# Three products of high and low parts as two matmuls: the down projections and the up projections of two SwiGLU stages

## The chip, the cores and the metric

The kernel runs on one core of a Trainium2 chip. The metric is the device time of one execution in microseconds (us), lower is better. The time before is the median of three runs, 1114.51 us (1113.62 to 1114.54).

## The reference, cut to what matters

One sequence of 256 tokens with 1024 features passes through three layers. Each ends in a feed-forward stage of width 2816 (22 blocks of 128):

```python
def conv_ffn(h, w_up, conv_w, conv_b, w_down):      # first layer: stage "1"
    a = causal_dwconv(h @ w_up, conv_w, conv_b)
    gate, val = jnp.split(a, 2, axis=-1)
    return (jax.nn.silu(gate) * val) @ w_down
def swiglu(h, w_gu, w_down):                        # second and third layer: stages "a" and "b"
    gate, up = jnp.split(h @ w_gu, 2, axis=-1)
    return (jax.nn.silu(gate) * up) @ w_down
```

All is float32. Ahead of the second layer's feed-forward stage stands its mixer, `x + concat([grouped, mem_out]) @ w_out`; its output product is called "outa" here.

## The kernel before, in words

Everything is kept feature-major: an array is [128 partitions, chunk of 128 features, 256 tokens]. Weights stream from HBM through four slots of a ring (`ring`, 1 MB each) on SyncE's queue (SP). The order of all work is one list of steps made by `order()` and walked by every engine: ("g", stage, i) is one group of a projection, 256 outputs wide, which fills one PSUM bank of 512 float32 columns (two halves of 128 outputs x 256 tokens); ("sq", ...), ("ns", ...) and ("nm", ...) are the squares, the sums over features and the reciprocal root of a norm.

**The split products.** For most projections a float32 product is made of three matmuls in the type float32r. A weight W is split into W_hi (ScalarE copies it with rounding, `high`, L1444) and W_lo = W - W_hi (VectorE, `low`, L1865), in halves of 1024 columns; two buffers of each (`w_hi`, `w_lo`) alternate. The activations have `xh`, `xl` in the same way. `three` (L938) then issues for each chunk k of 128 input features W_hi x_hi, W_hi x_lo and W_lo x_hi, each a matmul of 256 columns with a weight load of its own, all accumulated in the same 256 columns of PSUM. Call the three of one k a triple. ScalarE may overwrite buffer q%2 with weights q+2 only when the group that used q has ended (`grouped`), and TensorE starts group q+2 when VectorE has made its low part (`lo_ready`).

**The up products (`ffn`).** 22 groups in each stage: per group two halves (gate, value) of 8 triples. A group uses one of the four banks `banks[g % RING]`. VectorE then multiplies the bank by the norm's reciprocal root (L2257, 128x512, into `acc`), makes the next low weights, and in stages "a" and "b" waits for ScalarE's silu of the gate half (L1748), multiplies gate and value (L2280), rounds the product to `hid_hi` (L2283) and subtracts for `hid_lo` (L2285). In stage "1" GpSimd does these last three and VectorE does a convolution. The other four banks (S0, S1, T, O) serve scores, transposes, attention outputs and norm sums, and are idle in the feed-forward stages but for the norm's sums.

**The down products** (stage[:4] == "down"): 8 groups in each of the three stages, each of 22 triples in two halves of the weights (11 chunks, 128x1408), in 256 columns of a bank; VectorE adds the bank to x (L2060).

**outa** has four groups. They are not split: `feature_major` (L986) runs plain float32 matmuls on `mixa` and the ring's slot; each leaves two records of 256 columns in the trace. Group 0 is begun early.

**Norm sums.** VectorE adds the squares of four pairs of chunks to `total` (L2107, 128x512), folds the two halves of `total` together (L2111, 128x256), and TensorE multiplies by ones once (L1213).

Of the kernel before, what the change touches and what calls it, by code (L numbers as in the profile page):

```python
# [30 lines left out]
P = 128  # L31
# [214 lines left out]

BRANCHES = ("fox", "mla")
# [9 lines left out]
def order():  # L257
# [37 lines left out]
    st += [("row", "fox", 0), ("row", "fox", 1), ("g", "memkv", 1), ("keep",), ("nm", "m5"), ("sq", "m6")]  # L295
# [31 lines left out]
    def first_layer(heads):  # L327


        n = len(heads)  # L330
        out = [("G", *heads[0])]
        made, conv = [], []
        for t in range(n + 2):
            ssd = t < n and heads[t][0] == "ssd"
            ends = [heads[h] for h in (t - 2, t - 1) if h in range(n) and heads[h][1] % 2 and
                    (heads[h][0] == "ssd") == (h == t - 1)]
            out += starts(heads, t) + ([("B", *heads[t])] if ssd else [])
            out += [("sh", *g) for g in made[-1:]] + [("tn", *g) for g in conv]
            out += [("D", *h) for h in ends]
            out += [("C", *heads[t - 1])] if 1 <= t <= n else []  # L340
            out += [("B", *heads[t])] if t < n and not ssd else []
            out += [("sl", *g) for g in made[-1:]]
            out += [("P", *heads[t])] if t < n and not ssd else []
            out += [("fn", *g) for g in conv]
            out += [("L", *h) for h in ends if h[0] in BRANCHES]
            out += [("ev", *g) for g in made]
            out += [("G", *heads[t + 1])] if t + 1 < n else []
            conv = [g for g in made if g[0] == "xbc"]
            made = [g for g in dense[t] if len(g) == 2 and g[0] in TICKED]
            for g in dense[t]:  # L350
                if g[0] not in TICKED:
                    out.append(g)
                elif len(g) == 3:
                    out.append(("half", *g[:2]))
                else:
                    out.append(("g", *g))
                    if g != made[-1]:
                        out += [("sh", *g), ("sl", *g)]
            out += [("row", "ssd" if t else "fox", h) for h in rows_at.get(t, ())]
            out += {0: [("nm", "m6"), ("sq", "m7")], 1: [("nm", "m7")]}.get(t, [])  # L360
            for i, at in enumerate((26, 28, 30, 33)):
                if t == at:
                    out += [("hi", "ssm", i), ("sq", "ssm", i)] + ([("ns", "ssm", i)] if i < 3 else [])
        return out
# [8 lines left out]
    pool = [[("g", "pool", 1)], [("g", "pool", 0), ("pl", 0), ("g", "memkv", 2)], [("g", "wg", 2)], [("g", "wg", 1)],  # L373
            [("g", "wg", 0), ("early",)], [("g", "memkv", 3)]]
# [35 lines left out]
def number(steps):  # L410
# [4 lines left out]
    def one(stage, i):  # L415
        nonlocal g, l
        group[stage, i] = g
        key = load_key(stage, i)
        keys = [(stage, 2 * i), key] if stage[:4] == "down" else [key]
        for key in keys:  # L420
            if key not in load:
                load[key] = l
                l += 1
                if stage in SPLIT or stage[:2] == "up" or stage[:4] == "down":
                    split[key] = len(split)
            last[key] = g
        g += 1
# [96 lines left out]
def build(nc, cst_at, par_at, x_in, mem_in, pos_in, cst_in, cst2_in, par_in, w, out):  # L524
    with ExitStack() as ctx:
# [13 lines left out]
        xh = sb("xh", [P, KC, S], F32R)  # L539
        xl = sb("xl", [P, KC, S], F32R)  # L540
# [76 lines left out]
        hid_hi = zb("hid_hi", [P, NFF, S], F32R)  # L617
        hid_lo = zb("hid_lo", [P, NFF, S], F32R)
# [19 lines left out]
        zb("hole5", [P, (2 * NFF - 14) * S - 6 * 16])  # L638
# [54 lines left out]
        tapped = sem("tapped")  # L693
        stored = sem("stored")
# [103 lines left out]
        def halves_of(wide):  # L798
            return (0, wide // 2), (wide // 2, wide)

# [96 lines left out]
        def _(pe):  # L897
# [30 lines left out]
            def three(out, w_of, x_of, ks, wait=None, stationary=True, whole=True, start=True, **kw):  # L928


                for k in ks:
                    if wait is not None:
                        pe.wait_ge(*wait(k))
                    for a, b in ((0, 0), (0, 1), (1, 0)):
                        lhs, rhs = w_of(a, k), x_of(b, k)
                        if not stationary:
                            lhs, rhs = rhs, lhs
                        last = mm(out, lhs, rhs, start=(start and k == 0 and (a, b) == (0, 0)), **kw,  # L938
                                  stop=(whole and k == ks[-1] and (a, b) == (1, 0)))
                return last  # L940
# [103 lines left out]
            def group(stage, i, half=None):  # L1044
# [36 lines left out]
                elif stage[:4] == "down":  # L1081
                    base = FFN_BASE[stage[4]]
                    hidden = lambda k: (up_hid, base + k + 1)
                    for half in range(2):
                        parts = split_parts((stage, 2 * i + half))
                        last = three(banks[g % RING][:, 0:S],
                                     lambda a, k: parts[a][:, (k % HALF) * P:(k % HALF + 1) * P],
                                     lambda a, k: (hid_hi, hid_lo)[a][:, k, :],
                                     range(half * HALF, (half + 1) * HALF),
                                     hidden if i == 0 else None, whole=half == 1)  # L1090
# [52 lines left out]
                elif stage == "outa":  # L1143
# [4 lines left out]
                    else:  # L1148
                        last = feature_major(stage, i, W, KC, 256, two, lambda k: mixa[:, k, :])
# [18 lines left out]
            def ffn(name):  # L1168
                g0, q0 = GROUP["up" + name, 0], SPLITS["up" + name, 0]

                def up(u, it):
# [3 lines left out]
                    W = w_hi[:, q % 2, :], w_lo[:, q % 2, :]  # L1175
                    w_of = lambda m, a, k: W[a][:, k * 256 + m * P:k * 256 + (m + 1) * P]
# [8 lines left out]
                    last.then_inc(grouped, 1)  # L1185

# [8 lines left out]
            def total_sums(s):  # L1195
# [16 lines left out]
                pe.wait_ge(folded, n["totals"])  # L1212
# [206 lines left out]
        def _(act):  # L1419
# [296 lines left out]
            def ffn(name):  # L1716
                conv = name == "1"
                g0, n0, q0 = GROUP["up" + name, 0], LOAD["up" + name, 0], SPLITS["up" + name, 0]

                def up(j, u, it):  # L1720
# [13 lines left out]

                    parts()
                    act.wait_ge(free, it + (g // RING + 1))
# [34 lines left out]
            for s in STEPS:  # L1771
# [4 lines left out]
                elif s[0] == "tn":  # L1776
                    xbc_tanh(s[2])
                elif s[0] == "rest":
# [61 lines left out]
        def _(dve):  # L1840
# [127 lines left out]
            def group(stage, i):  # L1968
# [127 lines left out]
            def add_squares(name, i):  # L2096
# [12 lines left out]
                if i == 3:  # L2109
# [128 lines left out]
            def ffn(name):  # L2238
# [4 lines left out]
                def up(j, u, it):  # L2243
# [13 lines left out]
                    V.tensor_tensor(y.rearrange("p (a t) -> p a t", a=2), bank[:, :].rearrange("p (a t) -> p a t", a=2),  # L2257
                                    factor(S), ALU.mult).then_inc(free, 1)
# [28 lines left out]
                with dve.Fori(0, NFF // RING) as it:  # L2287
# [11 lines left out]
            for s in STEPS:  # L2299
# [4 lines left out]
                elif s[0] == "fn":  # L2304
                    xbc_finish(s[2])
                elif s[0] == "rest":
# [70 lines left out]
        def _(pool):  # L2377
# [25 lines left out]
            def up(j, u, it):  # L2403
# [4 lines left out]
                pool.wait_ge(up_silu, it * RING + (u + 1))  # L2408
                Q.tensor_tensor(h, sg[:, r, 0:S], acc[:, r, S:2 * S], ALU.mult).then_inc(hid_t, 1)  # L2409
                pool.wait_ge(hid_t, it * RING + (u + 1))  # L2410
                Q.tensor_copy(hi, h).then_inc(hid_high, 1)
                pool.wait_ge(hid_high, it * RING + (u + 1))
                Q.tensor_tensor(lo, h, hi, ALU.subtract).then_inc(up_hid, 1)

            for s in STEPS:
                if s[0] == "G":
                    decays(s)
                elif s == ("ffn", "1"):
                    with pool.Fori(0, NFF // RING) as it:
                        for u in range(RING):  # L2420
                            up(it * RING + u, u, it)
# [31 lines left out]
```

## Time and profile before

| what | value |
|---|---|
| median of three runs | 1114.51 us |
| the profiled execution's own time | 1113.32 us |
| its span, first to last instruction | 1111.5 us |
| TensorE busy | 1088.2 us (98%) |
| VectorE busy | 767.8 us (69%) |
| ScalarE busy | 599.5 us (54%) |
| GpSimd busy | 97.5 us (9%) |
| mean load of the DMA engines over the span | 172 GB/s |
| granted TensorE clock, mean | 0.997 |

Busy times are unions of spans in which an engine had an instruction under way. A matmul's own duration contains its fill and drain and overlaps its neighbours', so what one matmul costs is the distance from its start to the start of the next (its pitch), not the mean duration in a group's row. The chain is the work that ended last, followed back from the end of the program.

### The profile page before, as it was taken

To read this page: it belongs to the slowest core of one execution; us is meant where nothing else is said; L and a number is where in the kernel's file an instruction comes from. 1 tells how busy PE (TensorE), PEld (TensorE's weight loads), DVE (VectorE), ACT (ScalarE), POOL (GpSimd) and SP (SyncE) were. 2 spreads that over 40 slices of the span, in tenths; PEclk is the share of its full clock that TensorE was granted. 3 is DMA by queue.
4 is the path that set the end of the run, shared out by engine and by line. 5 is a ranking of instruction groups with operands and counts; after the bars stand their busy time and mean duration, and the time that the engine had idled before them with its cause. 6 is when DMAs were issued, how large, how long until landed. Compare 5 with 4: busy or idle time off the path is not lost.

```text
span 1111.5 us, 21454 instructions
## 1 busy us (share of the span) xinstructions
PE 1088.2 (98%) x8622; PEld 1039.4 (94%) x8622; DVE 767.8 (69%) x1213; ACT 599.5 (54%) x948; POOL 97.5 (9%) x112
## 2 busy tenths in 40 slices
PE   8999999999999999999999999999999999999997
PEld 8987899999999999999978999999999779999997
DVE  6855898678877999955744677756656446777643
ACT  6675667556646556544423444436657644444353
POOL 0000211055200433200000000000000000000000
PEclk9999999999999999999999999999999999999999
DMA  9445443556545556456524655445643136554451
GB/s 343 151 166 202 155 157 105 177 181 217 169 173 175 178 186 232 148 179 219 176 76 154 243 182 186 162 156 188 227 171 115 39 114 228 190 189 165 157 185 62
DMA packets 33905, 191.07 MB, mean 172 GB/s; under 512 B 3917, under 2 KB 7269, under 8 KB 16677
## 3 DMA queue, kind: packets, MB, share of 16 engines
q1 hardware_dynamic: 33252, 188.95, 48.7%
q10 hardware_dynamic: 576, 1.05, 0.3%
q8 instruction: 55, 0.90, 0.3%
q14 instruction: 22, 0.17, 0.0%
HBM read 187.86 MB, written 2.12 MB: 171 GB/s over the span
## 4 chain that ended last, share of the span: by engine, by line
PE 87%; DVE 7%; ACT 4%; issue 1%; DMA 1%; SPq 0%; DVEq 0%; ACTq 0%
PE bank L938 73%; PE bank L986 5%; DVE w_lo L1865 2%; PE bank L995 1%; PE O L1340 1%; ACT w_hi L1444 1%; PE S L1226 1%; PE bank L1020 1%; PE T L1313 1%; PE bank L1030 1%; ACT pr L1683 1%; DVE padu L1950 1%; DMA x<-x_in 1%; PE O L1345 0%; PE S L1248 0%
## 5 line engine op out<-in xcount | busy, mean ns | idle before, releaser
L1444 ACT ACTIVATE w_hi<-ring 128x1024 fp32r<-128x1024 f32 (+2 forms) x348 | 316.6, 957 | 329.7 <-PE bank L938 329.7
L938 PE MATMUL bank<-xh,w_hi 128*128 128x256 f32 x1600 | 452.9, 283 | 2.4 <-DVE w_lo L1865 1.6
L1865 DVE TENSOR_TENSOR w_lo<-ring,w_hi 128x1024 fp32r<-128x1024 f32 (+2 forms) x348 | 372.9, 1113 | 117.3 <-ACT w_hi L1444 116.4
L938 PE MATMUL bank<-xl,w_hi 128*128 128x256 f32 x1600 | 447.3, 280 | 0.0
L938 PE MATMUL bank<-xh,w_lo 128*128 128x256 f32 x1600 | 445.7, 279 | 0.0
L938 PEld LDWEIGHTS bank<-xh,w_hi 128*128 128x128 f32 x1600 | 300.6, 188 | 6.0 <-issue 4.2
L938 PEld LDWEIGHTS bank<-xl,w_hi 128*128 128x128 f32 x1600 | 300.9, 188 | 0.2
L938 PEld LDWEIGHTS bank<-xh,w_lo 128*128 128x128 f32 x1600 | 300.7, 188 | 0.0
L938 PE MATMUL bank<-hid_hi,w_hi 128*128 128x256 f32 x528 | 148.2, 281 | 0.5 <-DVE w_lo L1865 0.5
L938 PE MATMUL bank<-hid_lo,w_hi 128*128 128x256 f32 x528 | 148.1, 280 | 0.0
L938 PE MATMUL bank<-hid_hi,w_lo 128*128 128x256 f32 x528 | 148.1, 280 | 0.0
L938 PEld LDWEIGHTS bank<-hid_hi,w_hi 128*128 128x128 f32 x528 | 99.5, 188 | 0.7 <-issue 0.7
L938 PEld LDWEIGHTS bank<-hid_hi,w_lo 128*128 128x128 f32 x528 | 99.5, 188 | 0.0
L938 PEld LDWEIGHTS bank<-hid_lo,w_hi 128*128 128x128 f32 x528 | 99.5, 188 | 0.0
L2257 DVE TENSOR_TENSOR acc<-bank,rstd 128x512 f32<-128x512 f32 x44 | 30.4, 692 | 42.4 <-PE bank L938 35.4
L2267 DVE SCALAR_TENSOR_TENSOR acc<-pr,par,acc 128x255 f32<-128x255 f32 (+1 forms) x88 | 56.5, 681 | 3.0 <-DVE acc L2267 0.2
L1565 ACT ACTIVATE xh<-x,cst,par 128x256 fp32r<-128x256 f32 x40 | 21.8, 592 | 38.2 <-DVE x L2063 32.7
L2086 DVE SCALAR_TENSOR_TENSOR xl<-x,par,xh 128x256 fp32r<-128x256 f32 x40 | 17.6, 481 | 18.8 <-ACT xh L1565 18.8
L2409 POOL TENSOR_TENSOR sg<-sg,acc 128x256 f32<-128x256 f32 x20 | 17.1, 853 | 135.9 <-ACT sg L1753 135.9
L2063 DVE SCALAR_TENSOR_TENSOR x<-bank,x 128x512 f32<-128x512 f32 x12 | 8.3, 688 | 28.0 <-PE bank L1030 14.2
L2400 POOL TENSOR_SCALAR G<-mqk,sums 128x256 f32<-128x256 f32 x12 | 18.1, 1512 | 85.8 <-ACT pr L1660 49.2
L1742 ACT ACTIVATE acc<-pr,par 128x256 f32<-128x256 f32 x44 | 23.8, 588 | 0.0
(327 smaller groups left out, 1561.3 us busy)
## 6 DMA issues: line engine op xcount, KB each, us to landing
ring<-w_up SPq DMA_DIRECT2D x22, 1024.0 KB, 4.9
ring<-w_upa SPq DMA_DIRECT2D x22, 1024.0 KB, 4.8
ring<-w_upb SPq DMA_DIRECT2D x22, 1024.0 KB, 4.8
ring<-w_gate SPq DMA_DIRECT2D x12, 1024.0 KB, 4.9
ring<-w_down SPq DMA_DIRECT2D x16, 704.0 KB, 4.0
ring<-w_downa SPq DMA_DIRECT2D x16, 704.0 KB, 4.0
ring<-w_downb SPq DMA_DIRECT2D x16, 704.0 KB, 4.0
ring<-w_xbc SPq DMA_DIRECT2D x6, 1024.0 KB, 4.9
```

The source lines that it names most:

```text
L938: last = mm(out, lhs, rhs, start=(start and k == 0 and (a, b) == (0, 0)), **kw, stop=(whole and k == ks[-1] and (a, b) == (1, 0)))
L986: last = mm(b[p0:p0 + width, m * S:m * S + S], W[0:kp, k * wide + c0:k * wide + c0 + width], src(k), start=(k == 0), stop=(k == kc - 1))
L995: last = mm(b[:, tt * wide:(tt + 1) * wide], src(k)[:, tt * P:(tt + 1) * P], W[:, k * wide:(k + 1) * wide], start=(k == 0), stop=(k == kc ...
L1444: A(w_hi[:, q % 2, a:e], raw[:, a:e], ACT.Copy).then_inc(hi_ready, 1)
L1565: last = A(hi[:, c, :], src[:, c, :], ACT.Identity, bias=C("zero"), scale=Pm(gain, c))
L1742: last = A(acc[:, r, m * S:(m + 1) * S], pr[:, r, m * S:(m + 1) * S], ACT.Identity, bias=par[:, bass.ds(j * 8 + o + 3, 1)], scale=par[:, b ...
L1865: last = V.tensor_tensor(w_lo[:, q % 2, a:e], raw[:, a:e], w_hi[:, q % 2, a:e], ALU.subtract)
L2086: last = stt(lo[:, c, :], norm_io(name)[0][:, c, :], Pm(gain, c), hi[:, c, :], ALU.mult, ALU.subtract)
L2257: V.tensor_tensor(y.rearrange("p (a t) -> p a t", a=2), bank[:, :].rearrange("p (a t) -> p a t", a=2), factor(S), ALU.mult).then_inc(free, 1)
L2267: ins = stt(part, y[:, m * S:(m + 1) * S - late], par[:, bass.ds(j * 8 + o, 1)], part, ALU.mult, ALU.add)
L2400: Q.tensor_scalar(g[:, 0:S], R, c0, 0.0, ALU.add, ALU.min)
L2409: Q.tensor_tensor(h, sg[:, r, 0:S], acc[:, r, S:2 * S], ALU.mult).then_inc(hid_t, 1)
```

## The change

1. `two_wide` is new. For each k it issues one matmul W_hi [x_hi | x_lo] of 512 columns into a whole bank (x_hi's product in columns 0 to 255, x_lo's in 256 to 511), and one W_lo x_hi of 256 columns, accumulated on columns 0 to 255. The two halves of the bank are added behind it. `xh`, `xl` and `hid_hi`, `hid_lo` become halves of one array each. The down products of all stages and the up products of stages "a" and "b" use it.
2. An up group of stages "a" and "b" now needs two banks, one for each half: `banks[g % RING]` and `second_bank(u)` = (T, O, S0, S1)[u]. ScalarE copies columns 256 to 511 of both to `pr` (two copies, ahead of its next high weights), VectorE adds columns 0 to 255 of both to `pr` (two adds into `acc`) and then multiplies by the norm's factor. `down` gets a second add into x.
3. outa's groups 1 to 3 become split products with `three`; `mixa` gets `mixa_h` and `mixa_l` (new steps "mh": a copy on ScalarE, a subtraction on VectorE), and the three weights are split as others are.
4. The fold of `total` is left out for the norms ssm, ffn1 and mixb: TensorE sums two products instead of one. The squares and sums of norms m5, m6, m7 move ahead of a group of weights each.

```diff
+THREE = [("outa", i) for i in range(1, 4)]
+FOLDED = ("x1", "mem", "mixa", "ffna", "ffnb")
@@ order
-    st += [("row", "fox", 0), ("row", "fox", 1), ("g", "memkv", 1), ("keep",), ("nm", "m5"), ("sq", "m6")]
+    st += [("nm", "m5"), ("sq", "m6"), ("row", "fox", 0), ("row", "fox", 1), ("g", "memkv", 1), ("keep",)]
...
+            out += {0: [("nm", "m6"), ("sq", "m7")], 1: [("nm", "m7")]}.get(t, [])
             conv = [g for g in made if g[0] == "xbc"]
             made = [g for g in dense[t] if len(g) == 2 and g[0] in TICKED]
...
-            out += {0: [("nm", "m6"), ("sq", "m7")], 1: [("nm", "m7")]}.get(t, [])
...
-    pool = [[("g", "pool", 1)], [("g", "pool", 0), ("pl", 0), ("g", "memkv", 2)], [("g", "wg", 2)], [("g", "wg", 1)],
-            [("g", "wg", 0), ("early",)], [("g", "memkv", 3)]]
+    pool = [[("g", "pool", 1)], [("g", "pool", 0), ("pl", 0), ("g", "memkv", 2)], [("g", "wg", 2)], [("g", "wg", 1), ("mh", 2)],
+            [("g", "wg", 0), ("early",), ("mh", 1)], [("mh", 0), ("g", "memkv", 3), ("mh", 3)]]
@@ tensor
+            def two_wide(bank, w_of, x2_of, ks, wait=None, whole=True):
+                main, both = bank[:, 0:S], bank[:, :].rearrange("p (b t) -> p b t", b=2)
+                for k in ks:
+                    if wait is not None:
+                        pe.wait_ge(*wait(k))
+                    mm(both, w_of(0, k), x2_of(k), start=k == 0, stop=False, skip_group_check=True)
+                    last = mm(main, w_of(1, k), x2_of(k)[:, 0, :], start=False, stop=whole and k == ks[-1],
+                              skip_group_check=True)
+                return last
@@ down
-                        last = three(banks[g % RING][:, 0:S],
...
+                        last = two_wide(banks[g % RING],
+                                        lambda a, k: parts[a][:, (k % HALF) * P:(k % HALF + 1) * P],
+                                        lambda k: hid[:, :, k, :], range(half * HALF, (half + 1) * HALF),
+                                        hidden if i == 0 else None, whole=half == 1)
@@ outa
-                        last = feature_major(stage, i, W, KC, 256, two, lambda k: mixa[:, k, :])
+                        pe.wait_ge(mixa_lo, 4)
+                        last = feature3(stage, i, 256, two3, None, (mixa_h, mixa_l))
@@ norm sums
-                pe.wait_ge(folded, n["totals"])
+                if name not in FOLDED:
+                    pe.wait_ge(sq_added, 3 * n["totals"])
+                    product(sums_bank(name)[:, 0:S], [(C("ones"), total[:, c * S:(c + 1) * S]) for c in range(2)])\
+                        .then_inc(s_done, 1)
+                    return
@@ scalar, up
+                    if not conv:
+                        act.wait_ge(grouped, it * RING + (g + 1))
+                        for m, b in enumerate((bank, second_bank(u))):
+                            last = A(pr[:, r, m * S:(m + 1) * S], b[:, S:2 * S], ACT.Copy)
+                        last.then_inc(rest_copied, 1)
                     parts()
...
+                        act.wait_ge(scaled, it * RING + (base - NFF + u + 1))
@@ vector, down
-                    V.tensor_tensor(x[:, i, :], x[:, i, :], b[:, 0:S], ALU.add).then_inc(free, 1)
+                    own(V.tensor_tensor(x[:, i, :], x[:, i, :], b[:, 0:S], ALU.add))
+                    V.tensor_tensor(x[:, i, :], x[:, i, :], b[:, S:2 * S], ALU.add).then_inc(free, 1)
@@ vector, up of stages a and b
+                        dve.wait_ge(rest_copied, it * RING + (base - NFF + u + 1))
+                        if not (isinstance(j, int) and j < 2):
+                            dve.wait_ge(hid_t, it * RING + (base + u - 1))
+                        for m, b in enumerate((bank, second_bank(u))):
+                            last = V.tensor_tensor(y[:, m * S:(m + 1) * S], b[:, 0:S], pr[:, r, m * S:(m + 1) * S], ALU.add)
+                        last.then_inc(free, 1)
+                        dve.wait_ge(free, it + (g // RING + 1))
+                        y2 = y.rearrange("p (a t) -> p a t", a=2)
+                        V.tensor_tensor(y2, y2, factor(S), ALU.mult).then_inc(scaled, 1)
                     parts()
```

## Rows read from the trace of the kernel before

**Rows 1.** The page: busy time by engine; the chain that ended last, by line

```profile
PE 1088.2 (98%) x8622; PEld 1039.4 (94%) x8622; DVE 767.8 (69%) x1213; ACT 599.5 (54%) x948; POOL 97.5 (9%) x112
PE bank L938 73%; PE bank L986 5%; DVE w_lo L1865 2%; PE bank L995 1%; PE O L1340 1%; ACT w_hi L1444 1%; PE S L1226 1%; PE bank L1020 1%; PE T L1313 1%; PE bank L1030 1%; ACT pr L1683 1%; DVE padu L1950 1%; DMA x<-x_in 1%; PE O L1345 0%; PE S L1248 0%
```

**Rows 2.** Chain in order of time: start us, length us, what, instructions

```profile
47.38 0.86 PE S L1226 x2
...
588.96 20.72 PE bank L986 x96
...
615.72 181.39 PE bank L938 x1536
```

**Rows 3.** Timeline, stage a's up: start us, duration us, engine, instruction

```profile
639.93 0.28 PE L938 MATMUL bank<-xh,w_hi 128*128 128x256 f32 x1
639.94 0.19 PEld L938 LDWEIGHTS bank<-xl,w_hi 128*128 128x128 f32 x1
640.05 0.28 PE L938 MATMUL bank<-xl,w_hi 128*128 128x256 f32 x1
```

**Rows 4.** Timeline of weight loads around float32 matmuls of 128 columns (L1305, L1306)

```profile
822.54 0.41 PEld L1305 LDWEIGHTS S<-pr,cst 128*128 128x128 f32 x2
822.87 0.30 PEld L1306 LDWEIGHTS S<-pr,cst 128*128 128x128 f32 x2
823.09 0.19 PEld L938 LDWEIGHTS bank<-xh,w_hi 128*128 128x128 f32 x1
823.20 0.19 PEld L938 LDWEIGHTS bank<-xl,w_hi 128*128 128x128 f32 x1
```

**Rows 5.** Timeline, VectorE in stage a's up, one whole group and the next's start

```profile
649.67 0.69 DVE L2257 TENSOR_TENSOR acc<-bank,rstd 128x512 f32<-128x512 f32 x1 [0.86 <-PE bank L938]
650.77 2.36 DVE L1865 TENSOR_TENSOR w_lo<-ring,w_hi 128x1024 fp32r<-128x1024 f32 x2 [0.40 <-ACT w_hi L1444]
653.05 0.42 DVE L2280 TENSOR_TENSOR sg<-sg,acc 128x256 f32<-128x256 f32 x1
653.62 0.29 DVE L2283 CAST hid_hi<-sg 128x256 f32 x1 [0.16 <-DVE sg L2280]
654.04 0.42 DVE L2285 TENSOR_TENSOR hid_lo<-sg,hid_hi 128x256 f32 x1
655.33 0.69 DVE L2257 TENSOR_TENSOR acc<-bank,rstd 128x512 f32<-128x512 f32 x1 [0.86 <-PE bank L938]
```

**Rows 6.** Timeline, VectorE at the start of the stage, without waits between

```profile
617.05 0.69 DVE L2257 TENSOR_TENSOR acc<-bank,rstd 128x512 f32<-128x512 f32 x1 [3.53 <-ACT rstd L1636]
...
621.57 0.42 DVE L2285 TENSOR_TENSOR hid_lo<-sg,hid_hi 128x256 f32 x1
621.91 0.68 DVE L2257 TENSOR_TENSOR acc<-bank,rstd 128x512 f32<-128x512 f32 x1
622.56 2.36 DVE L1865 TENSOR_TENSOR w_lo<-ring,w_hi 128x1024 fp32r<-128x1024 f32 x2
```

**Rows 7.** Timeline, ScalarE in the same group as rows 5, and at the stage's start

```profile
618.75 1.28 ACT L1748 ACT_TABLE_LOAD   x1
...
649.67 2.01 ACT L1444 ACTIVATE w_hi<-ring 128x1024 fp32r<-128x1024 f32 x2 [3.25 <-PE bank L938]
651.59 0.49 ACT L1748 ACTIVATE sg<-acc,cst 128x256 f32<-128x256 f32 x1
```

**Rows 8.** By line, ns min/median/max: the down add; ScalarE's copy of 256 PSUM columns

```profile
L2060 DVE TENSOR_TENSOR x<-x,bank x24: 410/414/422, 477.8 to 1103.2; 128x256 f32<-128x256 f32 x24
...
L1714 ACT ACTIVATE mixa<-O x2: 384/384/384, 567.9 to 578.5; 128x256 f32<-128x256 f32 x2
```

**Rows 9.** Timeline and chain: m5's sums, the next scores; the fold of ffn1's sum

```profile
107.06 1.02 PE L1226 MATMUL S<-sqr,cst 96*128 96x512 f32 x2
108.91 0.49 PE L1287 MATMUL S<-fqk 64*128 64x128 f32 x4 [0.82 <-issue]
...
345.72 0.43 DVE lnv L2111
```

More of the change, by code:

```diff
@@ L423, in one @@
                 l += 1
-                if stage in SPLIT or stage[:2] == "up" or stage[:4] == "down":
+                if stage in SPLIT or key in THREE or stage[:2] == "up" or stage[:4] == "down":
                     split[key] = len(split)
@@ L1185, in up, with wide_up @@
                     last.then_inc(grouped, 1)
+                def wide_up(u, it, g, w_of):
+                    begin = isinstance(it, int) and it == 0
+                    after_t, after_s = (T_USE["rt",], S_USE["nm", "mixb"]) if name == "a" else \
+                        (len(T_USE), S_USE["nm", "last"])
+                    if begin and u == 0:
+                        pe.wait_ge(t_free, after_t)
+                    if begin and u == 1:
+                        pe.wait_ge(headed, O_USE["mema" if name == "a" else "memb", 1] + 1)
+                    if begin and u >= 2:
+                        pe.wait_ge(s_free[u - 2], (after_s - u + 3) // 2)
+                    both = banks[g % RING], second_bank(u)
+                    step = 2 if begin and u == 0 else KC
+                    for k0 in range(0, KC, step):
+                        for m in range(2):
+                            last = two_wide(both[m], lambda a, k: w_of(m, a, k), lambda k: xhl[:, :, k, :],
+                                            range(k0, k0 + step), after("ffn" + name) if step == 2 and m == 0 else None,
+                                            whole=k0 + step == KC)
+                    last.then_inc(grouped, 1)
+                    if step == 2:
+                        total_sums(("ns", "ffn" + name, 3))
                 for u in range(RING):
@@ L1777, in _ @@
                     xbc_tanh(s[2])
+                elif s[0] == "mh":
+                    if s[1] == 3:
+                        act.wait_ge(headed, O_USE["mema", 1] + 1)
+                    else:
+                        g = GROUP["wg", s[1]]
+                        act.wait_ge(evacuated[g % RING], g // RING + 1)
+                    A(flat(mixa_h[:, 2 * s[1]:2 * s[1] + 2, :]), flat(mixa[:, 2 * s[1]:2 * s[1] + 2, :]), ACT.Copy)\
+                        .then_inc(mixa_hi, 1)
                 elif s[0] == "rest":
@@ L2285, in hidden @@
                     V.tensor_tensor(lo, h, hi, ALU.subtract).then_inc(up_hid, 1)
-                with dve.Fori(0, NFF // RING) as it:
+                if not conv:
+                    for j in range(RING):
+                        up(j, j, 0)
+                with dve.Fori(0 if conv else 1, NFF // RING) as it:
                     for u in range(RING):
@@ L2305, in _ @@
                     xbc_finish(s[2])
+                elif s[0] == "mh":
+                    n["mixa"] += 1
+                    dve.wait_ge(mixa_hi, n["mixa"])
+                    V.tensor_tensor(pair(mixa_l, s[1]), pair(mixa, s[1]), pair(mixa_h, s[1]), ALU.subtract)\
+                        .then_inc(mixa_lo, 1)
                 elif s[0] == "rest":
```

51 lines of the change are left out of this document (33 added, 18 removed).

## The prediction

> **What bounds the kernel now.** I read the busy times and the chain first: TensorE is busy for 98% of the span, and 73% of the chain is the one line that issues the split products [rows 1]. Nothing but TensorE time, or a new wait of TensorE, can move the end much. Then I asked what one matmul costs. The chain in order of time has a piece of 181.39 us with 1536 matmuls of 256 columns, stage a's up and down products without a break [rows 2]: 181.39/1536 = 118.1 ns each, 354.3 ns for a triple and 48 x 118.1 = 5.66 us for an up group, the 5.66 us between VectorE's groups [rows 5].
>
> 256 columns at 2.4 GHz are 106.7 ns, so 11.4 ns of each 118.1 are something else, and the case turns on what. The timeline shows that a weight load starts when the matmul before it starts (639.94 beside 639.93), and the next matmul 0.12 us later [rows 3]: as if the load, not the columns, set the pitch. Two more rows bear on it. outa's float32 matmuls leave two records each, 20.72/96 = 215.8 ns a record, 213.3 of them columns, so where the load has time to hide only 2.5 ns are lost [rows 2]. The same holds for 512 columns: 0.86/2 = 430 ns against 426.7 [rows 2]. And loads under float32 records of 106.7 ns follow each other every (823.20 - 822.87)/3 = 110 ns [rows 4]. I read: pitch = the larger of columns + 2.5 ns and one load, 110 to 118 ns, and the load is 118 beside a float32r stream.
>
> **The pair.** Per k the change streams the same 768 columns with two loads for three. By that reading the 512-column matmul takes the 215.8 ns of a record with 213.3 ns of columns (its successor's load is hidden), and the 256-column one, over which the next load must run, 118.1. Pair 333.9 ns, saved 354.3 - 333.9 = 20.4 ns. There are 22 x 8 x 3 = 528 triples in the down products and 22 x 2 x 8 x 2 = 704 in the two up stages. Down: 10.8 us. Up: 14.4 us if TensorE stays the bound there; its group becomes 16 x 333.9 = 5.34 us. Bounds per k: nothing saved (everything grows with columns) and 28.5 ns (215.8 + 110).
>
> **VectorE in the up stages.** It now has 0.86 + 0.40 us idle in 5.66 [rows 5]. Its slot of new work, from starts without waits between: last subtraction to the next instruction 0.34, rounded to 0.40 for three waits computed there [rows 6]; two adds of 256 columns, which last as long as the down add, 0.41 [rows 8], at pitch 0.34 and then, since the multiplication waits for the second, 0.57 as between L2280 and L2283 [rows 5]; the multiplication of 512 columns 0.65 [rows 6]; both low parts 2.28 (653.05 - 650.77), then 0.57 and 0.42 for the hidden block [rows 5]. Sum 0.40 + 0.34 + 0.57 + 0.65 + 2.28 + 0.57 + 0.42 = 5.23 us, against 5.34 of TensorE. It fits with 0.1 us to spare. The wait for ScalarE's copies (two of 0.38 [rows 8], so 0.8 us after a group's end) costs nothing while VectorE is still in the group before at that moment: 0.8 + 5.23 = 6.03 ends 0.69 into the next, which it may start at 0.8. Low weights are ready 0.8 + 0.34 + 0.57 + 0.65 + 2.28 = 4.6 us after the group two before them ended, TensorE wants them at 5.34. The cover is thin; at a loop's end VectorE has more bookkeeping, and I take 0.7 us off for groups in which it is late. ScalarE has 2.01 + 0.49 of 5.66 [rows 7], plus 0.8: no bound. The second banks are idle in these stages: nothing.
>
> **Starts of the two up stages.** Low weights for group 2 were ready at 617.05 + 0.77 + 2.28 = 620.1 [rows 6] and TensorE's group 1 ended at 615.72 + 5.66 = 621.4 [rows 2]. New: copies 0.8, adds 0.9, so about 621.8, and group 1 ends at 621.1. The silu's table load of 1.28 us [rows 7] keeps VectorE's backlog. In stage a the weights of group 1 can be split only after outa's last group, because outa's groups now hold both buffers: ready some 6.3 us after its end, against a first group of 5.34 and the sums. I take 1.3 us lost for both stages; bounds 0 and 3.
>
> **outa.** 48 matmuls of 431.7 ns [rows 2] become 48 triples of 354.3: 3.7 us saved. Copies and subtractions for `mixa`, and the splits of three weights (2.01 us on ScalarE, 2.28 on VectorE each), lie beside the second layer's memory-value product (memkv 3) and outa 0, ten us in which both engines are nearly idle; the last pair waits for the attention's output and is done some 2 us after that product ends, 1.5 us before group 1. Nothing, and if that cover went, 1 us.
>
> **Small parts.** After m5's sums (107.06 + 0.86) TensorE stands until 108.91, 1.0 us [rows 9]; moved ahead of a group, the wait is hidden. m6 and m7 may give as much each, or move their wait elsewhere: I take 1.5 for the three, bounds -1 and 3. The fold that ffn1 loses (0.43 [rows 9]) stands before low weights for which TensorE waits: 0.4. In the other two norms the second product of 0.43 fills TensorE's idle time: nothing. The second down add (0.41 and a wait) shows only at the program's end, partly under TensorE's first sums: 0.3 lost; in the 23 others it lies under a group of 7.8 us.
>
> **Sum.** 10.8 + 14.4 - 0.7 - 1.3 + 3.7 + 1.5 + 0.4 - 0.3 = 28.5 us. The profiled execution took 1113.3 us (span 1111.5), 1.2 below the median; the same 28.5 off the median gives **1086.0 us**. About 0.2% (2.2 us) can be told from no change.
>
> **Rivals.**
> A, a fixed 11.4 ns for every float32r matmul whatever its length: the pair is 320 + 22.8 = 342.8, saved 11.4 x 1232 = 14.0; with the rest (3.7 + 1.9 - 0.3) and 1.0 for starts, 18.3: 1096.2. For it: no float32r matmul in the trace has another length. Against it: the float32 records lose only 2.5. Chance 0.15.
> B, the extra grows with columns but for 2.5 ns: a float32r stream reads slower than 2.4 GHz. The pair is 351.8, saved 2.5 x 1232 = 3.1; in all 7.9: 1106.6. Against it only that loads and starts go in step [rows 3]. Chance 0.08. The Trainium skill, page "TensorE: Matmul & The Clock Gate", section "Back-to-back issue gap", speaks for so small a gain: it puts a warm matmul at columns/2.4 ns + 2.5 with nothing for the load, so two instead of three save 2.5 ns. Its 109.2 ns for 256 columns disagree with the 118.1 measured here.
> C, VectorE becomes the bound of the up stages: four more waits at some 0.1 us each that don't hide would make its slot 5.65, and the up products gain nothing: 10.8 + 3.7 + 1.6 - 2.0 = 14.1: 1100.4. For it: 0.1 us to spare. Chance 0.15.
> D, slower: VectorE waits in every group for ScalarE's copies and does all its work behind them, slot 0.8 + 5.23 + 0.1 = 6.1 us; 44 x (6.1 - 5.66) = 19.4 lost against 14.1 gained elsewhere: 1119.8. It decides from a slot of 5.66 + 14.1/44 = 5.98. Against it: TensorE's next group runs while VectorE works, so the copies are made in VectorE's shadow. Chance 0.05.
>
> **The numbers.** Forecast 0.54, A 0.15, B 0.08, C 0.15, D 0.05, and 0.03 for less still than all bounds. Low end: pair of 326, down 528 x 28.5 = 15.0, up held by VectorE at 5.25, 44 x 0.41 - 2 = 16.0, and 5.3 for the rest: 36.3, so 1078. High end: C and A inside, B and D left out: 1103. Faster 0.91, same 0.03, slower 0.06.
>
> **What would show it.** In the profile after: a 512-column float32r matmul and the start after it 0.216 us apart, the next pair's start 0.118 later; 342.8 in sum would be A, 352 B. Up groups 5.34 us apart on TensorE without waits for w_lo; C shows as such waits and VectorE over 98% busy at a longer period; D as VectorE waiting for ScalarE's `pr` in each group. Down groups of 22 x 0.334 = 7.35 us instead of 7.79. outa's three groups 17.0 us instead of 20.7. The prediction is wrong if the pair doesn't cost 334, or VectorE's slot exceeds 5.34.

## The result and the profile after

The changed kernel takes 1108.26 us (median of five runs, 1107.72 to 1108.64) against 1114.54 us for the kernel before (five runs on the same chip, 1113.62 to 1115.53): ratio 0.9942, 95% interval 0.993 to 0.9955, 6.3 us less. The forecast was 1086.0 in 1078 to 1103. The direction is right, the size is not: 6.3 us came for 28.5.

The page of the changed kernel, the lines that answer to [rows 1], and three of its groups of instructions (count | busy us, mean ns | idle before, what ended it):

```profile
PE 1080.5 (98%) x7444; PEld 980.5 (89%) x7444; DVE 815.1 (74%) x1332; ACT 632.8 (57%) x1046; POOL 98.7 (9%) x112
...
L960 PE MATMUL bank<-hid,w_hi 128*128 128x512 f32 x528 | 184.9, 394 | 3.3 <-DVE w_lo L1938 2.9
L961 PE MATMUL bank<-hid,w_lo 128*128 128x256 f32 x528 | 147.8, 280 | 0.0
...
L2339 DVE TENSOR_TENSOR acc<-bank,pr 128x256 f32<-128x256 f32 x44 | 18.7, 425 | 26.8 <-ACT pr L1793 26.8
```

TensorE is still busy 98% of the span. 1178 matmul records fewer stand in it (8622 to 7444: the third matmuls of 1232 triples, while outa's exchange adds 48 and the norms' second products 6), and the span is 5.6 us shorter (1105.9 against 1111.5). So 1178 fewer matmuls brought little, and the first question is what the new pair costs. The timeline of stage a's up answers to [rows 3]:

```profile
640.14 0.39 PE L960 MATMUL bank<-xhl,w_hi 128*128 128x512 f32 x1
640.14 0.19 PEld L961 LDWEIGHTS bank<-xhl,w_lo 128*128 128x128 f32 x1
640.37 0.28 PE L961 MATMUL bank<-xhl,w_lo 128*128 128x256 f32 x1
640.37 0.19 PEld L960 LDWEIGHTS bank<-xhl,w_hi 128*128 128x128 f32 x1
640.49 0.39 PE L960 MATMUL bank<-xhl,w_hi 128*128 128x512 f32 x1
```

The wide matmul starts at 640.14, the narrow one at 640.37, the next wide one at 640.49. By the medians over the stage that is 228 and 118 ns (229 to 230 and 117 in the down stages), and from pair to pair 346.7 ns on average in all five stages. The narrow one is as forecast. The wide one is 12 to 14 ns dearer than the 215.8 forecast, though the load under it (0.19 us, begun with it) ended before it did. The triples of the same stages took 353.3 ns in stage a's up, 350.0 in stage b's, and 356.0, 356.0 and 352.0 in the down products of stages 1, a and b. So the pair saves 6.7 and 3.3 ns in up and 9.3, 9.3 and 5.3 in down, not 20.4.

The timeline of VectorE in the same stage, the answer to [rows 5]:

```profile
639.74 0.42 DVE L2339 TENSOR_TENSOR acc<-bank,pr 128x256 f32<-128x256 f32 x1 [0.45 <-ACT pr L1793]
640.08 0.41 DVE L2339 TENSOR_TENSOR acc<-O,pr 128x256 f32<-128x256 f32 x1
640.52 0.69 DVE L2343 TENSOR_TENSOR acc<-acc,rstd 128x512 f32<-128x512 f32 x1
641.13 2.35 DVE L1938 TENSOR_TENSOR w_lo<-ring,w_hi 128x1024 fp32r<-128x1024 f32 x2
643.41 0.42 DVE L2365 TENSOR_TENSOR sg<-sg,acc 128x256 f32<-128x256 f32 x1
643.97 0.29 DVE L2368 CAST hid<-sg 128x256 f32 x1
644.40 0.43 DVE L2370 TENSOR_TENSOR hid<-sg,hid 128x256 f32 x1
645.19 0.42 DVE L2339 TENSOR_TENSOR acc<-bank,pr 128x256 f32<-128x256 f32 x1 [0.37 <-ACT pr L1793]
```

From 639.74 to 645.19 less 0.37 of idle time is a slot of 5.08 us; the groups come every 5.55 us. VectorE waits 0.4 us in each of these two groups. TensorE waits for low weights only at stage a's second group (below), nowhere further inside these stages.

The second finding is in the down stages, where TensorE waited only at the start before. The timeline of TensorE in the changed kernel's stage 1 down, where a first half of weights ends:

```profile
503.12 0.39 PE L960 MATMUL bank<-hid,w_hi 128*128 128x512 f32 x1
503.35 0.28 PE L961 MATMUL bank<-hid,w_lo 128*128 128x256 f32 x1
503.87 0.47 PE L960 MATMUL bank<-hid,w_hi 128*128 128x512 f32 x1 [0.24 <-DVE w_lo L1938]
504.18 0.28 PE L961 MATMUL bank<-hid,w_lo 128*128 128x256 f32 x1
```

The timeline of ScalarE in the same kernel, ahead of that stop:

```profile
496.10 1.48 ACT L1498 ACTIVATE w_hi<-ring 128x704 fp32r<-128x704 f32 x2 [2.34 <-PE bank L961]
499.50 1.10 ACT L1619 ACTIVATE xhl<-x,cst,par 128x256 fp32r<-128x256 f32 x2 [1.93 <-DVE x L2134]
500.50 0.71 ACT L1659 ACTIVATE sqr<-x,cst 128x512 f32<-128x512 f32 x1
501.12 1.46 ACT L1498 ACTIVATE w_hi<-ring 128x704 fp32r<-128x704 f32 x2
```

And that of VectorE:

```profile
496.93 1.69 DVE L1938 TENSOR_TENSOR w_lo<-ring,w_hi 128x704 fp32r<-128x704 f32 x2 [2.12 <-ACT w_hi L1498]
498.54 0.41 DVE L2133 TENSOR_TENSOR x<-x,bank 128x256 f32<-128x256 f32 x1
498.99 0.42 DVE L2134 TENSOR_TENSOR x<-x,bank 128x256 f32<-128x256 f32 x1
500.63 0.88 DVE L2160 SCALAR_TENSOR_TENSOR xhl<-x,par,xhl 128x256 fp32r<-128x256 f32 x2 [1.23 <-ACT xhl L1619]
501.43 0.69 DVE L2181 TENSOR_TENSOR lnv<-sqr 128x512 f32<-128x512 f32 x1
502.03 1.69 DVE L1938 TENSOR_TENSOR w_lo<-ring,w_hi 128x704 fp32r<-128x704 f32 x2
```

Read it backwards. TensorE's pair at 503.87 waits for the low weights begun at 502.03. These could begin only with the high weights of 501.12, which stand in ScalarE's order behind `xhl` and the squares, which wait for the second add into x (498.99), which VectorE does behind the low weights of 496.93. A stop and the slow first pair behind it cost 0.4 to 0.5 us. There are three in each down stage, nine in all: by the spacing of the starts 4.2 us, as much as the pair saves there (176 x 9.3 + 176 x 9.3 + 176 x 5.3 ns = 4.2 us).

The kernel before had room at this place. In its stage a, VectorE's low weights ended at 755.57 + 1.69 = 757.26, and TensorE's first matmul of the half that uses them began at 757.77 (timeline of both engines):

```profile
755.57 1.69 DVE L1865 TENSOR_TENSOR w_lo<-ring,w_hi 128x704 fp32r<-128x704 f32 x2 [0.41 <-ACT w_hi L1444]
...
757.77 0.28 PE L938 MATMUL bank<-hid_hi,w_hi 128*128 128x256 f32 x1
```

This 0.5 us of room stands against the 0.45 us of the second add and the 0.2 us by which 22 pairs are shorter than 22 triples (22 x 9.3 ns).

The third is a stop of TensorE in front of stage a's second up group, which the kernel before did not have (the same kernel's timeline of TensorE):

```profile
609.07 0.59 PE L1267 MATMUL S<-lnv,cst 128*128 128x256 f32 x2
610.91 0.50 PE L960 MATMUL bank<-xhl,w_hi 128*128 128x512 f32 x1 [1.24 <-DVE w_lo L1938]
```

### The profile page after: what moved, and what is told of

It is laid out like the page before. It is cut to its first block, busy times and chain, and to the rows that moved or that the text cites. A ratio compares the mean times of both kernels' runs of the same rounds, so it can differ in the third digit from the quotient of the medians.

```text
span 1105.9 us, 19448 instructions
## 1 busy us (share of the span) xinstructions
PE 1080.5 (98%) x7444; PEld 980.5 (89%) x7444; DVE 815.1 (74%) x1332; ACT 632.8 (57%) x1046; POOL 98.7 (9%) x112
## 4 chain that ended last, share of the span: by engine, by line
PE 70%; DVE 16%; ACT 7%; issue 5%; DMA 1%; DVEq 1%; SPq 0%; ACTq 0%
PE bank L949 26%; PE bank L960 14%; PE bank L961 7%; DVE w_lo L1938 7%; DVE acc L2352 3%; PE S L960 3%; PE bank L1009 3%; ACT w_hi L1498 2%; PE O L960 2%; PE T L960 2%; PE S L961 2%; PE bank L1018 1%; PE O L1394 1%; PE O L961 1%; DVE pr L2332 1%
## 5 line engine op out<-in xcount | busy, mean ns | idle before, releaser
L949 PE MATMUL bank<-xhl,w_hi 128*128 128x256 f32 x1792 | 321.0, 282 | 1.9 <-DVE w_lo L1938 1.5
L949 PEld LDWEIGHTS bank<-xhl,w_hi 128*128 128x128 f32 x1792 | 273.4, 188 | 6.3 <-issue 4.9
L949 PE MATMUL bank<-xhl,w_lo 128*128 128x256 f32 x896 | 250.3, 279 | 0.0
L960 PE MATMUL bank<-hid,w_hi 128*128 128x512 f32 x528 | 184.9, 394 | 3.3 <-DVE w_lo L1938 2.9
L949 PEld LDWEIGHTS bank<-xhl,w_lo 128*128 128x128 f32 x896 | 168.8, 188 | 0.0
L961 PE MATMUL bank<-hid,w_lo 128*128 128x256 f32 x528 | 147.8, 280 | 0.0
L960 PE MATMUL bank<-xhl,w_hi 128*128 128x512 f32 x352 | 124.9, 392 | 1.3 <-DVE w_lo L1938 1.2
L960 PEld LDWEIGHTS bank<-hid,w_hi 128*128 128x128 f32 x528 | 99.2, 188 | 28.5 <-issue 6.0
L961 PE MATMUL bank<-xhl,w_lo 128*128 128x256 f32 x352 | 99.3, 282 | 0.0
L961 PEld LDWEIGHTS bank<-hid,w_lo 128*128 128x128 f32 x528 | 99.2, 188 | 0.0
L960 PEld LDWEIGHTS bank<-xhl,w_hi 128*128 128x128 f32 x352 | 66.1, 188 | 15.7 <-DVE w_lo L1938 2.0
L961 PEld LDWEIGHTS bank<-xhl,w_lo 128*128 128x128 f32 x352 | 66.7, 190 | 0.1
L960 PE MATMUL S<-xhl,w_hi 128*128 128x512 f32 x160 | 56.3, 390 | 0.0
```

Source lines behind the costliest of these rows:

```text
L960: mm(both, w_of(0, k), x2_of(k), start=k == 0, stop=False, skip_group_check=True)
L961: last = mm(main, w_of(1, k), x2_of(k)[:, 0, :], start=False, stop=whole and k == ks[-1], skip_group_check=True)
```

## The experiments

Theory S: the pair is cheaper by only some 3 to 9 ns; the down edit gives its gain back in the nine stops, and outa's in part in the stop at stage a's start. All times are medians; the kernel before took 1114.42 us on the chip of experiments 1 to 4, 1114.65 on that of 5 and 7 to 9, 1114.15 on that of 6.

**1. The down products undone.** `two_wide` in down back to `three`, one add into x.

```diff
-                        last = two_wide(banks[g % RING], ...
+                        last = three(banks[g % RING][:, 0:S], ...
...
-                    own(V.tensor_tensor(x[:, i, :], x[:, i, :], b[:, 0:S], ALU.add))
-                    V.tensor_tensor(x[:, i, :], x[:, i, :], b[:, S:2 * S], ALU.add).then_inc(free, 1)
+                    V.tensor_tensor(x[:, i, :], x[:, i, :], b[:, 0:S], ALU.add).then_inc(free, 1)
```

> The down products are undone (three matmuls, one add into x); the rest of the change stays. Theory S: the new down products gain 8 ns a pair (356 to 348 in the trace after), 528 x 8 = 4.2 us, and give back more than that, because TensorE stands three times in each of the three down stages for low weights (9 stops, 0.50 us longer than a pitch each, 4.5 us, with the slow first pair behind each 5.2); undone, the time stays within 1.5 us of the changed kernel's 1108.3, and the nine stops are gone. Rival R (the stops are not caused by the down edit, but by noise in other engines): undone, the stops stay and the time rises by 4 us to 1112.

Measured: 1106.99 us (ratio to before 0.9932, 0.9918 to 0.9945), 1.3 us less than with the down edit, inside the 1.5 that theory S allowed, and no stops within the down stages; in its groups of instructions by line, the down products wait only at the start of a stage, as in the kernel before:

```profile
L949 PE MATMUL bank<-hid,w_hi 128*128 128x256 f32 x1056 | 188.6, 281 | 0.5 <-DVE w_lo L1939 0.5
L949 PE MATMUL bank<-hid,w_lo 128*128 128x256 f32 x528 | 148.3, 281 | 0.0
```

The two intervals of the ratio overlap, so the 1.3 us alone would be thin. The traces say the same: from first to last down matmul the three stages take 188.9 us in sum here and 189.3 in the changed kernel, and the end of the program behind the last one takes 8.8 us here and 9.4 there. As it stands, the edit in the down products earns nothing and costs up to 1.3 us. Theory S holds.

**2. The up products undone.** `wide_up` isn't called, ScalarE's copies, VectorE's two adds and the wait between are taken out, the multiplication reads the bank again.

> The up products of stages a and b are undone (three matmuls, one multiplication); the rest of the change stays. Theory S: TensorE saves in the changed kernel 353.3 - 346.6 = 6.7 ns a pair in stage a and 350.6 - 346.6 = 4 ns in stage b, 352 pairs each, 3.8 us, and loses 1.6 us at the start of stage a to weights split late, part of which is due to the shorter first group; undone, the time rises by 2 to 4 us, to 1110.3 to 1112.3. Rival R (VectorE's longer slot holds the up stages back, so the up edit is worth nothing): undone, the time is 1108 or lower.

Measured: 1111.07 us (0.9969, 0.9957 to 0.9981), 2.8 us more than the changed kernel. The up edit is worth 2.8 us, within the 2 to 4 of theory S. The stop at stage a's start is as long without it (1.6 us between the starts around it), so the shorter first group has no part in it; that guess of mine falls.

**3. The adds ahead of the second low part.** Nothing is left out; only VectorE's order in a down group changes.

```diff
@@ vector, splits(g, behind=None, only=None)
+                    if only is not None and (BY_SPLIT[q - 2] in HALVES) != only:
+                        continue
@@ vector, group
-                    splits(GROUP[stage, i])
+                    splits(GROUP[stage, i], only=True if stage[:4] == "down" else None)
...
                     V.tensor_tensor(x[:, i, :], x[:, i, :], b[:, S:2 * S], ALU.add).then_inc(free, 1)
+                    splits(GROUP[stage, i], only=False)
```

> The changed kernel, but in each down group VectorE makes the low part that waits for the group's first half, then the two adds into x, then the low part that waits for the whole group; nothing is left out. Theory S: the two adds stood behind a low part that waits 0.8 us for ScalarE and takes 1.6, so ScalarE's high activations and squares, and the high weights behind them in its order, came late by the time of the second add; with the adds first all this comes 2 us earlier and the nine stops go: 4.5 to 5.2 us less, 1103.1 to 1103.8. Rival R (the stops come from ScalarE's order alone or from the DMAs): the stops stay, 1108.

Measured: 1104.14 us (0.9907, 0.9892 to 0.9923), 4.1 us less than the changed kernel, 0.3 above the range that theory S gave. Its timeline of VectorE at the same place:

```profile
496.06 0.42 DVE L2135 TENSOR_TENSOR x<-x,bank 128x256 f32<-128x256 f32 x1 [1.23 <-PE bank L961]
496.51 0.42 DVE L2136 TENSOR_TENSOR x<-x,bank 128x256 f32<-128x256 f32 x1
496.94 1.70 DVE L1938 TENSOR_TENSOR w_lo<-ring,w_hi 128x704 fp32r<-128x704 f32 x2
498.61 0.88 DVE L2163 SCALAR_TENSOR_TENSOR xhl<-x,par,xhl 128x256 fp32r<-128x256 f32 x2
499.41 0.69 DVE L2184 TENSOR_TENSOR lnv<-sqr 128x512 f32<-128x512 f32 x1
500.75 1.69 DVE L1938 TENSOR_TENSOR w_lo<-ring,w_hi 128x704 fp32r<-128x704 f32 x2 [0.66 <-ACT w_hi L1498]
```

The adds fill time in which VectorE waited for ScalarE (0.42 us at 496.51 where it stood idle before), the low weights still begin at 496.94, and the next ones at 500.75, not 502.03. The nine stops are gone; TensorE's wait for low weights before wide down matmuls falls from 2.9 us to 1.1, which is the start of stage 1's down, in the groups by line of this kernel:

```profile
L960 PE MATMUL bank<-hid,w_hi 128*128 128x512 f32 x528 | 183.8, 392 | 1.3 <-DVE w_lo L1938 1.1
```

The nine stops are shown to come from VectorE's order: nothing but that order was changed. With this order the down edit is worth 1106.99 - 1104.14 = 2.9 us. How the slack used up divides between the second add and the shorter group was not tested by itself.

**4. Other widths.** To see why the wide matmul costs 229 ns: in groups 1 to 7 of the down stages an unbroken moving operand and other numbers of columns. This kernel and those of experiments 5 and 6 replace or leave out down products, so they don't compute the layers. Each was run once and is read for its pitches alone.

```diff
+                            wide, narrow = {"1": (512, 256), "a": (512, 128), "b": (384, 256)}[stage[4]]
...
+                                k2 = min(k, NFF - 2)
+                                x2 = hid[:, 0, k2:k2 + 2, :].rearrange("p a t -> p (a t)")
+                                mm(banks[g % RING][:, 0:wide], parts[0][:, at], x2[:, 0:wide], ...
+                                last = mm(banks[g % RING][:, 0:narrow], parts[1][:, at], x2[:, 0:narrow], ...
```

> In groups 1 to 7 of the down stages the moving operand of the wide matmul is one unbroken stretch (hid_hi of k and k+1) in place of hid_hi and hid_lo of k, 22528 bytes apart; widths are 512 and 256 in stage 1, 512 and 128 in stage a, 384 and 256 in stage b. This leaves out or replaces part of the down products. Theory P (each float32r matmul costs 5.5 ns and 0.4375 ns a column, whatever the load): 512 takes 229.5 ns, 256 117.5, 384 173.5, 128 61.5, and the unbroken stretch changes nothing. Theory L (a load is a floor of some 118 ns, and beyond it columns/2.4 + 2.5): 128 takes 118, 384 162.5; and then the 229 ns of the wide matmul come from its broken operand and fall to 216. Theory F (11.4 fixed): 512 224.7, 384 171.4, 128 64.7.

Its timeline of TensorE in stage a's down (512 and 128) and stage b's (384 and 256):

```profile
759.79 0.44 PE L1120 MATMUL bank<-hid,w_hi 128*128 128x512 f32 x1
760.07 0.22 PE L1122 MATMUL bank<-hid,w_lo 128*128 128x128 f32 x1
760.13 0.44 PE L1120 MATMUL bank<-hid,w_hi 128*128 128x512 f32 x1
...
1059.66 0.34 PE L1120 MATMUL bank<-hid,w_hi 128*128 128x384 f32 x1
1059.84 0.28 PE L1122 MATMUL bank<-hid,w_lo 128*128 128x256 f32 x1
1059.96 0.34 PE L1120 MATMUL bank<-hid,w_hi 128*128 128x384 f32 x1
```

No theory is right as a whole. The unbroken stretch changes nothing (512 takes 230 in stage 1). 384 columns take 176.5, that is 16.5 above their 160.0 (at 2.4 GHz; the granted clock was 1.00 there), as 512 take 16.7 above 213.3. So between 384 and 512 columns the extra does not grow. And the pair of 512 and 128 takes 340 (759.79 to 760.13), of which the trace puts only 58 to the narrow one: 340 - 230 = 110, the interval of loads in [rows 4]. So theory L's floor is there, at 110 and not 118, for the narrow matmul.

**5. More widths.** The same edit with 512 alone, 256 and 256, 512 and 192.

> As the run widths, with other widths in groups 1 to 7 of the down stages: 512 alone in stage 1 (the matmuls with W_lo are left out), 256 and 256 in stage a, 512 and 192 in stage b. Theory F2 (a float32r matmul costs columns/2.4 plus a fixed 16.6 ns above 256 columns and 11 ns at 256, and a weight load is a floor of 110 ns, which the pair of 512 and 128 met with 230 + 110): 512 alone takes 230; 256 and 256 118 each; 512 and 192 together 340, the load's floor, not 230 + 91. Theory P (5.5 ns and 0.4375 ns a column, no floor): 229.5; 117.5 each; 229.5 + 89.5 = 319.

Measured: 512 and 192 take 1060.62 to 1061.99 for four pairs, 343 ns each (345 by the median over the stage): 3 to 5 above the floor's 340, far from P's 319. 256 and 256 take 118 to 119 each. 512 alone takes 234 by the median over stage 1's down (231 to 238), 4 more than theory F2 said. P falls. The timeline of TensorE at 512 and 192:

```profile
1060.62 0.42 PE L1120 MATMUL bank<-hid,w_hi 128*128 128x512 f32 x1
1060.87 0.25 PE L1123 MATMUL bank<-hid,w_lo 128*128 128x192 f32 x1
...
1061.99 0.42 PE L1120 MATMUL bank<-hid,w_hi 128*128 128x512 f32 x1
```

**6. Two banks, and 320 and 448 columns.** The narrow matmul of stage 1's down goes to the idle bank T.

> As the run widths (unbroken moving operand, groups 1 to 7 of the down stages); widths are 512 and 256 in stage 1, where the matmul with W_lo now accumulates in the idle bank T instead of the bank of its neighbour, 320 and 256 in stage a, 448 and 256 in stage b. This replaces part of the down products. Theory F2 (columns/2.4 plus a fixed 16.6 ns above 256 columns, wherever it goes): 512 takes 230, 320 150, 448 203. Rival D (the 16.6 ns are two matmuls after each other on one bank): 512 takes 216 in stage 1, and the other two as under F2. Theory P (5.5 ns and 0.4375 a column): 229.5, 145.5, 201.5.

Measured: 512 takes 230 in stage 1 all the same (490.75 to 490.98), so the extra is not owed to two matmuls on one bank; rival D falls. 448 take 204 (186.7 + 17) and 320 take 147.5 (133.3 + 14).

These kernels also show what the extra is not. In experiment 5 the granted clock fell to 0.5, that is 1.2 GHz, in short stretches from 486.3, 742.3 and 769.6, and in experiment 6 from 778.5. TensorE had stood for 1.9 to 2.2 us, waiting for low weights, just before each of them or at its beginning. The timeline of TensorE in experiment 6:

```profile
778.70 0.47 PE L1120 MATMUL bank<-hid,w_hi 128*128 128x320 f32 x1
778.96 0.41 PE L1123 MATMUL bank<-hid,w_lo 128*128 128x256 f32 x1
779.18 0.47 PE L1120 MATMUL bank<-hid,w_hi 128*128 128x320 f32 x1
```

There 320 columns take 266.5 ns (266.7 at 1.2 GHz) and 256 take 213.5 (213.3), and in experiment 5 512 take 427 (426.7). At 1.2 GHz the extra is gone. So it is neither a fixed time for each matmul nor a fixed number of TensorE's clocks. What causes the 11 to 17 ns that a float32r matmul takes beyond its columns at 2.4 GHz, where a float32 record takes 2.5 [rows 2], stays open. For the wide matmul a load as a floor, the operand's form and the bank are ruled out. Whether the change of weights itself costs it was not tested, since each float32r matmul here had its own load.

**7. outa undone.**

```diff
-THREE = [("outa", i) for i in range(1, 4)]
+THREE = []
...
-                        pe.wait_ge(mixa_lo, 4)
-                        last = feature3(stage, i, 256, two3, None, (mixa_h, mixa_l))
+                        last = feature_major(stage, i, W, KC, 256, two, lambda k: mixa[:, k, :])
```

> outa's split products are undone (float32 matmuls on mixa again, no splits of its weights, no steps mh); the rest of the change stays. Theory S: outa costs 3.7 us more on TensorE (23.99 against 20.26 in the stage), and the 1.6 us in which TensorE stands behind the first up group of stage a go, because the weights of the second up group can again be split during outa: together 2.1 us more than the changed kernel, 1110.4. Rival R (the stop at the start of stage a comes from the norm and from ScalarE's copies): the stop stays, 1112.0.

Measured: 1109.91 us, 1.65 more than the changed kernel, where theory S said 2.1. From outa's first late matmul to the first up matmul it is 23.99 us against 20.26, the 3.7 forecast; and the stop of 1.6 us at stage a's start is gone. Theory S holds: the weights of the second up group could be split only after outa's last group, because outa's weights held both buffers.

**8. Both repairs.** The order of experiment 3, and outa's last group in float32 (`THREE` with groups 1 and 2).

> The order of the adds as in down_order, and outa's last group in float32 again (groups 1 and 2 split). Theory S: the last group costs 16 x 78 ns = 1.2 us more, the stop of 1.6 us at the start of stage a goes: 0.4 us less than down_order, 1103.7. Rival R (the stop stays): 1105.4.

Measured: 1103.91 us (0.9903, 0.9887 to 0.9918). The stop is gone, and the dearer group takes nearly all of it back: 0.2 us less than experiment 3, which the runs cannot tell from nothing. It is the fastest kernel of the study, 10.7 us under the kernel before.

**9. The small parts alone.** Down, up and outa undone.

> Down, up and outa are undone; what is left of the change is the order of norms m5, m6, m7 and the fold left out for ssm, ffn1 and mixb. Theory S: TensorE reached stage 1 2.8 us earlier in the changed kernel (345.7 against 348.5), and the start of kk lost 0.3 us less: 1111.3. Rival R (that difference between two executions came from elsewhere): 1114.4, no difference.

Measured: 1111.9 us (0.9974, 0.9965 to 0.9983), 2.8 less than before, where theory S said 3.1. The scores that stood at 108.91 in [rows 9] now follow the matmul ahead of them at once, and m6's sums have a short stop in their place (timeline of TensorE in the changed kernel, which has these parts too):

```profile
107.67 0.49 PE L1341 MATMUL S<-fqk 64*128 64x128 f32 x4
107.99 0.60 PE L1343 MATMUL S<-fqk 64*128 64x256 f32 x4
109.33 1.10 PE L1280 MATMUL S<-sqr,cst 96*128 96x512 f32 x2 [0.73 <-DVE sc L2268]
```

Of three stops of 1.2 to 1.5 us between starts, one of 1.1 is left.

## Why the prediction was wrong, point by point

**The pair (down 10.8 us, up 14.4 us): the step that failed.** It put the wide matmul at "the 215.8 ns of a record with 213.3 ns of columns", taken from float32 records, as if the type did not matter. Measured: 228 to 230. The reading that pitch is the larger of columns and load was half right: a load is a floor of 110 ns (experiments 4 and 5), but a float32r matmul of 256 columns takes 117 to 119 and of 512 takes 228 to 230 by itself. The forecast left 13.9 ns of a pair beyond its columns (2.5 and 11.4); 26.7 were measured. The pair saves 9.3, 9.3 and 5.3 ns in down and 6.7 and 3.3 in up: 4.2 + 3.5 = 7.7 us where 25.2 were forecast, 17.5 of the 22.2 us missed. Rival A, an extra for each matmul whatever its length, had the form nearly right, and the doubt behind it was the right one ("no float32r matmul in the trace has another length"); its 342.8 ns are still 4 too low, since the extra is 11 at 256 columns and 15 to 17 at 512. A row of another type should have counted as a bound, not as the value. B's 351.8 was 5 too high; its total of 1106.6 came nearest to the measured time, by too small a saving and without the stops, so partly by luck. The range ended at 1103 and so left out the case that came nearest. The Trainium skill, page "TensorE: Matmul & The Clock Gate", section "Back-to-back issue gap", gives for a single matmul by itself a gap of columns/2.4 ns + 2.5, 215.8 ns for 512 columns. The float32r matmuls here disagree (228 to 230); a float32 record with as much column time agrees (215.8). Its section "LDWEIGHTS (loading the stationary operand)" gives columns/1.2 ns, 106.7 ns for a load of 128 columns; the floor measured here is 110.

**The second down add: the other step that failed.** I wrote that in the 23 other groups "it lies under a group of 7.8 us" and named TensorE's group as the cover. The cover that counts is the slack of the chain through ScalarE's order: add, high activations, squares, then the high weights of the next half, then their low part. The add of 0.45 us and TensorE's group shortened by 0.2 us used that slack of 0.5 us up in every second group. The nine stops cost 4.2 us by the spacing of starts, and experiment 3 took 4.1 back by the order alone. At the program's end the forecast was 0.3 us; the last down matmul stands 8.7 us before the end in the kernel before and 9.4 in the changed one, 0.7 more.

**VectorE in the up stages.** Forecast 5.23 us a slot, measured 5.08: right, each term within 0.04 us but for the pitch of the second add, 0.44 and not 0.57. With the group at 5.55 and not 5.34 it had more room than I thought. Rivals C and D are refuted: TensorE has no wait for low weights inside those stages behind the start. The sign named for D did show, since VectorE waits for `pr` 43 times in 44 groups, but the wait is slack in a slot of 5.08 us, not work in one of 6.1.

**Starts.** 1.3 us were forecast for both stages; it is one stop of 1.6 in stage a, all of it from outa's hold on the buffers (experiment 7). The forecast named that cause, but its figures (ready 6.3 us after outa, against a first group of 5.34 and the sums) give it only half a microsecond. Experiment 2 refutes a part of the shorter group in it. Not forecast at all: TensorE also loses more at the starts of the down stages, by the spacing of starts 2.3 us in the three against 0.8 before. The kernel of experiment 9, which has the old down products, already loses 1.4 there, so the down edit is only part of the cause; the rest stays open.

**outa.** 3.7 us forecast, 3.7 measured in the stage; net of the stop 1.65.

**Small parts.** 1.9 forecast for order and fold, 2.8 measured, inside the bounds.

The parts undone one at a time come to up 2.8, down -1.3, outa 1.65, the rest 2.8, together 5.9 of the 6.3 us. No part is known better than to about 1 us, and the traces show why: the same triples have more than one pitch. In stage 1's up, which no kernel here touches, a triple takes 353.3 ns in four kernels (the one before and those of experiments 1, 2 and 4) and 350.0 in the other seven, 118.83 against 117.71 us for the same 1008 matmuls. In stage b's up it takes 350.0 in the kernel before and 353.3 with the up edit undone; in stage b's down 352.0 before and 356.2 with the down edit undone. What sets it stays open. The step of 3.3 ns is as large as all that the pair saves in stage b's up. Differences below 1 us between two kernels are not read.

## What to carry to other kernels

Price a matmul from rows of its own type and, where none has the new width, treat the row of another type as an end of the range. When several loads are merged into one, ask which part of the pitch is the load's: only what exceeds the columns and the matmul's own extra comes back. And where an instruction is added on an engine that is half idle, follow what stands behind it in the order of each engine up to the bounding one: the second add cost nothing by VectorE's share and 4 us by its place, and moving both adds into VectorE's wait a few lines earlier took them back.

## What the runs showed of the hardware that was not expected

At a granted clock of 1.00 (2.4 GHz) a float32r matmul costs more than its columns by 10 to 12 ns at 256 columns (117 to 119), 14 at 320 (147.5), and 15 to 17 at 384, 448 and 512 (176.5, 204, 228 to 230), while a float32 record of 213.3 or 426.7 ns of columns costs 2.5 to 3.3 more [rows 2]. At a granted clock of 0.5 (1.2 GHz) the same matmuls take their columns and nothing more: 213.5 ns for 256, 266.5 for 320, 427 for 512. So the lower clock costs less than a factor of two there (427 against 230).

A matmul of 128 or 192 columns behind one of 512 leaves the pair at 340 and 343 to 345 ns, against 346.7 with 256 columns. So below 256 columns fewer columns save almost nothing: the next weight load needs 110. The starts that the trace gives to such short matmuls (58 ns before the next at 128 columns) don't show that; only the sum over the pair does.

Three float32r matmuls of 256 columns have a pitch of 350.0 ns in one kernel and 353.3 in another, over a whole stage and for the same instructions, at the same granted clock of 1.00.
